# Activations in two tiles, weight copies placed by foresight, and 16-column products alternating with 512-column ones

## The chip, the cores and the metric

One Trainium2 chip, one core. The time is the device time of one execution of the whole kernel in microseconds, the median of several runs.

## The reference

Two transformer-like blocks over 1024 tokens of width 1024, all in float32. The first block puts 16 learned tokens ahead (1040 in all), and computes differential attention beside a state space model, both from one projection:

```python
h = rms_norm(h_res, pre_mix_g)
proj = h @ w_in                       # q1 q2 k1 k2 (partial rope), v, u
o = rms_norm(diff_attention(q1, q2, k1, k2, v, lam), subln_g) * (1 - lam_init)
y = gelu(s5_ssm(u, ...)); y = rms_norm(y * sigmoid(y @ w_glu + b_glu), ssm_out_g)
h_res = h_res + rms_norm(concat(o, y) @ w_out, post_mix_g)
h = rms_norm(h_res, pre_ffn_g)
h_res = h_res + rms_norm((silu(h @ w_gate) * (h @ w_up)) @ w_down, post_ffn_g)
```

The second block works on the 1024 tokens alone: retention beside RWKV-7, an output product, a gated feed-forward of the same kind, and at the end a gated per-layer input. Every dense product is against a weight matrix with 1024 rows (2816 in w_down).

## The kernel before, in words

**Number format.** A float32 operand is held as a high part rounded to the fast format fp32r and a low part (the rest, in the same format). A product is three matmuls by PASSES: high weights by high activations, high weights by low activations, low weights by high activations (L144). The activations of all 1040 tokens are in act_hi and act_lo, each [128, 8, 1040], placed at byte 16512 of a partition one behind the other (L93, L94): row stride 4160 bytes, the first half of the tokens 64 bytes into a row, the second 2048 bytes further.

**Weights.** All weights come as 408 units of 512 KB, [128, 1024], in an order fixed in advance (ORDER), through six slots. SyncE starts the transfer of unit pos into w_raw as soon as TensorE has finished unit pos − 6 (L565 to L570). From unit 30 on (W_START) ScalarE rounds it into w_hi (round_to, L1467; its copy is recorded at the helper's line L697), and GpSimd makes w_lo = w_raw − w_hi (split_to, L577; recorded at L586). TensorE waits for w_lo (w_ready) before the unit's first product. Before unit 30 GpSimd makes both.

**Order of the work.** The text of each engine is written out in one fixed order. Tokens are treated in two halves of 512. Stage 0 (until 560 us) has the first block's norm, projection (project, L1545, then project_far, L1561, whose pieces are mixed with attention), the state space model and attention of half 0. Then come four phases, in each of which a mixing part of one half (attention, or retention and RWKV) is interleaved with a dense part of the other: phase 1 from 561 us, phase 2 from 1196, phase 3 from 2005, and phase 4 (the last dense part alone) from 2900 us. A list of events, EVENTS[1] to EVENTS[4] (L535 to L556), says whether the next step is mixing or dense. Each engine walks the same list: it does its own part of the event and, on ScalarE and GpSimd, then prepares weight units up to a number that the list gives for this event (L1508 to L1517 and L671 to L675). That number is the smaller of "units begun with this event, plus 3" (W_AHEAD) and "units ended three events earlier, plus 6". So a unit is prepared as soon as its slot can have been filled. A list event of a dense product is one quarter of a unit, six matmuls of 512 columns.

**Lines of products.** feature_product (L1610; matmuls at L1617) makes the q and k features of the first projection: per tile m of 128 features eight k steps times three passes, for 512 tokens (s=0) and, for m = 4 to 7, also for the 16 learned tokens (s=2). far_inputs (L1581, L1587) makes the four tiles of u in the same way. rotate (L1635, matmul L1640) makes rope's rotated half from ScalarE's copy qk_raw, which VectorE then combines. dense_products (L1848, matmuls L1855) has weights as stationary operand and activations as moving one; down (matmuls L1884) has the feed-forward's inner values ffh as stationary and weights as moving; token_product (L1891, L1896) has activations stationary and weights moving. Each product's result is copied out of PSUM by ScalarE or VectorE; before a PSUM bank is written again, TensorE waits for the copy (proj_kept in the projection).

**GpSimd's other work.** Besides splitting weights it makes tables at the start, and, in phases 2 and 3, helps RWKV: rw_keys (L600) waits for a transfer of aa and does seven multiplications, all recorded at L598, at 16 places of the list. It stands in GpSimd's order like any event.

Of the kernel before, what the change touches and what calls it, by code (L numbers as in the profile page):

```python
# [14 lines left out]
P = 128  # L15
# [70 lines left out]
def build(nc, t):  # L86
# [6 lines left out]
    act_hi = place("act_hi", [P, KT, L], F32R, AT_ACT)  # L93
    act_lo = place("act_lo", [P, KT, L], F32R, AT_ACT + KT * L * 4)  # L94
# [15 lines left out]
    def tok_cols(i):  # L110
        return slice(META + P * i, META + P * i + P)

# [6 lines left out]
    NEAR = META + BANK  # L119

# [24 lines left out]
    acts, ws = (act_hi, act_lo), (w_hi, w_lo)  # L145
# [411 lines left out]
    assert ended[-1] == len(ORDER)  # L557
    AT = {key: pos for pos, key in enumerate(ORDER)}
# [121 lines left out]
    def _(act):  # L680
# [42 lines left out]
        def first_norm():  # L723

            tiles = tiles_of(0)
            for step in range(len(tiles) + 2):
# [8 lines left out]
                if step >= 2:  # L735
                    g, rows, _, c0 = tiles[step - 2]
                    act.wait_ge(turned, g + 1)
                    if rows == META:
                        give(fn(act_hi[:, :, 0:META], ps[:, 0, 0:KT * META].rearrange("p (k n) -> p k n", k=KT), ACT.Copy), hi_done)
                    else:  # L740
                        for b in range(2):
                            bank = 2 * (g % 2) + b
                            fin = fn(act_hi[:, 4 * b:4 * b + 4, c0:c0 + P], ps[:, bank, :].rearrange("p (k n) -> p k n", k=4), ACT.Copy)
# [187 lines left out]
        def attention(h):  # L931

            def output_high(u):
                pair, qi, hh = unit_of(h, u)
                act.wait_ge(o_turned, HEAD_UNITS * h + u + 1)
                give(fn(act_hi[:, 2 * pair + hh, tok_cols(qi)], ps[:, 7, VD:2 * VD], ACT.Copy), o_hi)
# [43 lines left out]
        def glu(h):  # L980
# [36 lines left out]
            cols = slice(META + BANK * h, META + BANK * h + BANK)  # L1017
            for m in range(4):
                act.wait_ge(glu_prod, 4 * (2 * h + 1) + m + 1)
                give(fn(act_hi[:, 4 + m, cols].rearrange("p (c t) -> p t c", t=OCT), y_raw[:, m], ACT.Copy), glu_hi)  # L1020
# [24 lines left out]
        def mix_norm(h):  # L1045
# [3 lines left out]
            for step in range(NORM_STEPS):  # L1049
# [18 lines left out]
                if step >= 2:  # L1068
                    k = step - 2
                    act.wait_ge(dense_turned, gt_ + k + 1)  # L1070
                    for b in range(2):
                        out = act_hi[:, 4 * b:4 * b + 4, tok_cols(HALF * h + k)]
# [13 lines left out]
        def residual_half(h):  # L1086
# [12 lines left out]
            for step in range(NORM_STEPS):  # L1099
# [17 lines left out]
                if step >= 2:  # L1117
                    g, _, _, c0 = tiles[step - 2]
                    act.wait_ge(turned, g + 1)
                    for b in range(2):  # L1120
                        fin = fn(act_hi[:, 4 * b:4 * b + 4, c0:c0 + P], ps[:, 4 + 2 * (g % 2) + b, :].rearrange("p (k n) -> p k n", k=4), ACT.Copy)
# [101 lines left out]
        def ret_high(i):  # L1223
            act.wait_ge(ret_turned, i + 1)
            give(fn(act_hi[:, 0:4, tok_cols(i)], ps[:, 6, :].rearrange("p (k n) -> p k n", k=4), ACT.Copy), ret_hi)
# [2000 lines left out]
```

## Time and profile before

| what | value |
|---|---|
| median of 3 runs | 3389.66 us (3388.5 to 3397.58) |
| the profiled execution | 3409.39 us, span 3407.6 us |
| mean granted clock of TensorE | 0.943 |
| instructions | 48139, of them 19536 matmuls |
| bytes read from and written to HBM | 281.89 and 44.97 MB, 96 GB/s over the span |

PE is TensorE's matmuls, PEld its weight loads, DVE VectorE, ACT ScalarE, POOL GpSimd, SP SyncE. A profile row of a group gives line, engine, operation, destination and sources by the program's names, count, busy time and mean duration, and after the bar the time that the engine stood idle just before such instructions with what ended most of it. The duration of a matmul is modelled and overlaps with the next; the distance from start to start is its price. The granted clock is 1 at full speed (2.4 GHz) and 0.5 at the lower level (1.2 GHz).

### The profile page before, as it was taken

To read this page: it belongs to the slowest core of one execution; us is meant where nothing else is said; L and a number is where in the kernel's file an instruction comes from. 1 tells how busy PE (TensorE), PEld (TensorE's weight loads), DVE (VectorE), ACT (ScalarE), POOL (GpSimd) and SP (SyncE) were. 2 spreads that over 40 slices of the span, in tenths; PEclk is the share of its full clock that TensorE was granted. 3 is DMA by queue.
4 is the path that set the end of the run, shared out by engine and by line. 5 is a ranking of instruction groups with operands and counts; after the bars stand their busy time and mean duration, and the time that the engine had idled before them with its cause. 6 is when DMAs were issued, how large, how long until landed. Compare 5 with 4: busy or idle time off the path is not lost.

```text
span 3407.6 us, 48139 instructions
## 1 busy us (share of the span) xinstructions
PE 3105.6 (91%) x19536; PEld 2396.3 (70%) x19536; DVE 1506.9 (44%) x2264; ACT 1225.1 (36%) x1969; POOL 1232.6 (36%) x698
## 2 busy tenths in 40 slices
PE   6997877898998889989999989998999989899997
PEld 4775655676766666877777767777777767788875
DVE  5844542443443461355555553435455554222233
ACT  3111214533432463243444344343434443322232
POOL 5811302132322323434444332434444432344432
PEclk9887888899999889999999999999999989999998
DMA  4343323222212254332222243332222222322231
GB/s 152 118 119 94 104 78 106 87 74 87 69 62 71 77 187 152 103 99 86 75 76 84 72 155 133 129 103 81 84 74 86 78 72 82 123 93 96 90 105 56
DMA packets 158030, 330.02 MB, mean 97 GB/s; under 512 B 34960, under 2 KB 74064, under 8 KB 157808
## 3 DMA queue, kind: packets, MB, share of 16 engines
q1 hardware_dynamic: 58752, 213.94, 18.8%
q10 hardware_dynamic: 99056, 112.99, 10.2%
q8 instruction: 155, 2.54, 0.3%
q14 instruction: 67, 0.55, 0.0%
HBM read 281.89 MB, written 44.97 MB: 96 GB/s over the span
## 4 chain that ended last, share of the span: by engine, by line
PE 79%; DVE 12%; ACT 3%; ACTq 2%; issue 2%; DMA 1%; POOL 0%; DVEq 0%; POOLq 0%
PE ps L1855 34%; PE ps L1896 13%; PE ps L1884 12%; PE ps L1706 2%; PE ps L1617 2%; DVE acc_dense L2291 2%; PE ps L1587 1%; DVE ffh_lo L2971 1%; PE ps L2090 1%; ACTq L988 1%; PE ps L1627 1%; DVE act_lo L2291 1%; PE ps L1734 1%; PE ps L1794 1%; PE ps L1982 1%
## 5 line engine op out<-in xcount | busy, mean ns | idle before, releaser
L586 POOL TENSOR_TENSOR w_lo<-w_raw,w_hi 128x1024 fp32r<-128x1024 f32 x408 | 999.5, 2460 | 1735.1 <-ACT w_hi L697 1731.4
L1855 PE MATMUL ps<-act_hi,w_hi 128*128 128x512 f32 x1696 | 701.5, 414 | 13.6 <-ACT qk_raw L697 8.1
L1855 PE MATMUL ps<-act_lo,w_hi 128*128 128x512 f32 x1696 | 677.2, 399 | 0.0
L1855 PE MATMUL ps<-act_hi,w_lo 128*128 128x512 f32 x1696 | 673.6, 397 | 0.0
L697 ACT ACTIVATE w_hi<-w_raw 128x1024 fp32r<-128x1024 f32 x378 | 390.2, 1052 | 152.8 <-DMA w_raw<-weights 75.2
L1855 PEld LDWEIGHTS ps<-act_hi,w_hi 128*128 128x128 f32 x1696 | 322.5, 190 | 108.4 <-issue 16.6
L1855 PEld LDWEIGHTS ps<-act_hi,w_lo 128*128 128x128 f32 x1696 | 323.0, 190 | 74.6
L1855 PEld LDWEIGHTS ps<-act_lo,w_hi 128*128 128x128 f32 x1696 | 322.5, 190 | 66.7 <-issue 1.7
L1884 PE MATMUL ps<-w_hi,ffh_hi 128*128 128x512 f32 x704 | 297.2, 422 | 60.8 <-DVE acc_dense L2291 57.4
L2291 DVE TENSOR_TENSOR acc_dense<-acc_dense,ps 128x512 f32<-128x512 f32 x352 | 242.1, 688 | 228.5 <-PE ps L1884 182.3
L1896 PE MATMUL ps<-w_hi,act_hi 128*128 128x512 f32 x640 | 261.5, 409 | 26.7 <-POOL w_lo L586 11.9
L1884 PE MATMUL ps<-w_hi,ffh_lo 128*128 128x512 f32 x704 | 284.0, 403 | 0.0
L1884 PE MATMUL ps<-w_lo,ffh_hi 128*128 128x512 f32 x704 | 283.0, 402 | 0.0
L1896 PE MATMUL ps<-w_hi,act_lo 128*128 128x512 f32 x640 | 258.0, 403 | 0.0
L1896 PE MATMUL ps<-w_lo,act_hi 128*128 128x512 f32 x640 | 255.3, 399 | 0.0
L2967 DVE TENSOR_TENSOR ff_f<-ff_f,ps 128x512 f32<-128x512 f32 x88 | 60.5, 688 | 392.0 <-PE ps L1855 391.4
L1884 PEld LDWEIGHTS ps<-w_hi,ffh_hi 128*128 128x128 f32 x704 | 137.6, 195 | 103.1 <-DVE acc_dense L2291 65.8
L692 ACT ACT_TABLE_LOAD x141 | 180.9, 1283 | 32.8 <-issue 24.5
L1896 PEld LDWEIGHTS ps<-w_hi,act_hi 128*128 128x128 f32 x640 | 123.7, 193 | 61.1 <-issue 21.9
L1884 PEld LDWEIGHTS ps<-w_lo,ffh_hi 128*128 128x128 f32 x704 | 137.5, 195 | 31.2
L697 ACT ACTIVATE ff_f<-ps 128x512 f32<-128x512 f32 x88 | 52.7, 598 | 291.0 <-PE ps L1855 289.8
L1884 PEld LDWEIGHTS ps<-w_hi,ffh_lo 128*128 128x128 f32 x704 | 137.7, 196 | 25.9
(372 smaller groups left out, 4284.7 us busy)
## 6 DMA issues: line engine op xcount, KB each, us to landing
w_raw<-weights SPq DMA_DIRECT2D x408, 512.0 KB, 3.5
rw<-rw_t ACTq DMA_DIRECT2D x24, 256.0 KB, 2.3
rw<-lora_t ACTq DMA_DIRECT2D x24, 256.0 KB, 2.0
row<-x ACTq DMA_DIRECT2D x8, 512.0 KB, 3.7
row_dense<-x ACTq DMA_DIRECT2D x8, 512.0 KB, 6.1
row_mix<-res ACTq DMA_DIRECT2D x8, 512.0 KB, 8.0
res<-row_mix ACTq DMA_DIRECT2D x8, 512.0 KB, 4.2
acc_dense<-res ACTq DMA_DIRECT2D x8, 512.0 KB, 5.2
```

What stands on the lines that cost most here:

```text
L586: pool.tensor_tensor(w_lo[:, s], raw, w_hi[:, s].bitcast(F32), SUB).then_inc(w_ready, 1)
L692: act.preload_act_table_set(SETS[func])
L697: return act.activation(out, in_, func, **kw)
L988: act.dma_start(y_raw[SG * j:SG * j + SG, m], y_view[:, :, 8 * m + j, c0:c0 + BANK // OCT]).then_inc(y_landed, 16)
L1587: mm = pe.matmul(ps[:, n % 2, 0:c1 - c0], ws[w][:, pos % SLOTS, P * k:P * k + P], acts[a][:, k, c0:c1], start=(k, w, a) == (0, 0, 0), stop ...
L1617: mm = pe.matmul(ps[:, n % 3, 0:c1 - c0], ws[w][:, u % SLOTS, P * k:P * k + P], acts[a][:, k, c0:c1], start=(k, w, a) == (0, 0, 0), stop=( ...
L1706: mm = pe.matmul(out[:, c:c + w], q, k[:, META + c:META + c + w], start=True, stop=True)
L1855: mm = pe.matmul(out, ws[w][:, s, P * k:P * k + P], acts[a][:, k, x], start=(k, w, a) == (0, 0, 0), stop=(k, w, a) == (KT - 1, 1, 0))
L1884: mm = pe.matmul(ps[:, 2 + n % 2, :], ffh[a][:, m % 4, P * k:P * k + P], ws[w][:, s, BANK * j:BANK * j + BANK], start=(m % 2, w, a) == (0, ...
L1896: mm = pe.matmul(ps[:, kinds[2] + k, :], source[a][:, 2 * uu + kk, x], ws[w][:, pos % SLOTS, BANK * kk:BANK * kk + BANK], start=(uu, kk, w ...
L2291: give(dve.tensor_tensor(out, a, b, op), signal)
L2967: give(dve.tensor_tensor(ff_f[:, m % 2], ff_f[:, m % 2], ps[:, 1, :], MUL), ff_prod)
```

## The change

1. **Layout.** act_hi and act_lo are replaced by tiles in the same bytes: for the first block's projection near_hi and near_lo, [128, 8, 528], hold the 16 learned and the first 512 tokens, and half_acts[h], [128, 8, 512], hold a half each. half_acts[0] overlays the near tiles (it is written when they are done with). All reads and writes of activations go through these.
2. **Copies with foresight.** The number of units that ScalarE and GpSimd prepare after an event is worked out with a look at the units that begin up to six events later.
3. **Alternation.** feature_products and far_inputs make the 512-column and the 16-column product of a tile together, changing from one to the other at each weight tile; PE's waits for a free bank move accordingly.

The core of the diff:

```diff
-    act_hi = place("act_hi", [P, KT, L], F32R, AT_ACT)
-    act_lo = place("act_lo", [P, KT, L], F32R, AT_ACT + KT * L * 4)
+    near_acts, half_acts = [], ([], [])
+    for n, name in enumerate(("hi", "lo")):
+        at = AT_ACT + n * KT * L * 4
+        near_acts.append(place(f"near_{name}", [P, KT, NEAR], F32R, at))
+        for h in range(2):
+            half_acts[h].append(place(f"act_{name}_{h}", [P, KT, BANK], F32R, at + h * KT * NEAR * 4))
...
-    W_START, W_AHEAD, W_BEHIND = len(ORDER), 3, 4
-    EVENTS, ended, made_ready = {}, [W_START] * W_BEHIND, [W_START + W_AHEAD]
+    W_START, W_AHEAD, W_BEHIND, W_LOOK = len(ORDER), 3, 3, 6
+    EVENTS, begun, ended = {}, [], [W_START] * W_BEHIND
     def event(side, h, starts, ends):
         ORDER.extend((h, u) for u in starts)
-        assert len(ORDER) <= made_ready[-1]
+        begun.append(len(ORDER))
         ended.append(ended[-1] + len(ends))
-        made_ready.append(min(len(ORDER) + W_AHEAD, ended[-W_BEHIND] + SLOTS))
-        return side, made_ready[-1]
+        return side, len(begun) - 1
+
+    def weights_by(e):
+        soon = begun[min(e + W_LOOK, len(begun) - 1)]
+        return max(begun[min(e + 1, len(begun) - 1)], min(soon, begun[e] + W_AHEAD, ended[e + 1] + SLOTS))
...
             for n, (kind, m, s) in enumerate(PROJ):
-                if n >= 3:
-                    pe.wait_ge(proj_kept, n - 2)
+                ahead = len(spans_of(m)) - 1 if kind == "qk" else 0
+                if n + ahead >= 3 and s != 2:
+                    pe.wait_ge(proj_kept, n + ahead - 2)
                 if kind == "v":
                     value_product(n, m)
-                else:
-                    feature_product(n, m, s)
+                elif s != 2:
+                    feature_products(n, m)
...
-                free = len(PROJ) + n - (kind != "qk")
-                if n:
+                free = len(PROJ) + n - (kind != "qk" and s != 0)
+                if n and s != 2:
                     pe.wait_ge(proj_kept, free)
...
-            for k in range(KT) if s == 2 else range(2 * part, 2 * part + 2):
+            for k in range(2 * part, 2 * part + 2):
                 for w, a in PASSES:
-                    mm = pe.matmul(ps[:, n % 2, 0:c1 - c0], ws[w][:, pos % SLOTS, P * k:P * k + P], acts[a][:, k, c0:c1],
-                                   start=(k, w, a) == (0, 0, 0), stop=(k, w, a) == (KT - 1, 1, 0))
-            if s == 2 or part == 3:
-                post(mm, unit_done if s == 1 else proj_psum)
+                    for of, (c0, c1) in enumerate((SPANS[0], SPANS[2]) if s == 0 else (SPANS[1],)):
+                        mm = pe.matmul(ps[:, (n + of) % 2, 0:c1 - c0], ws[w][:, pos % SLOTS, P * k:P * k + P], first_cols(a, k, c0, c1 - c0),
+                                       start=(k, w, a) == (0, 0, 0), stop=(k, w, a) == (KT - 1, 1, 0))
+                        if (k, w, a) == (KT - 1, 1, 0):
+                            post(mm, unit_done if s == 1 else proj_psum)
...
-        def feature_product(n, m, s):
-
-            u, (c0, c1) = AT[0, U_QK + m], SPANS[s]
-            if s == 0:
-                pe.wait_ge(w_ready, u + 1)
+        def feature_products(n, m):
+
+            u = AT[0, U_QK + m]
+            pe.wait_ge(w_ready, u + 1)
             for k in range(KT):
                 for w, a in PASSES:
-                    mm = pe.matmul(ps[:, n % 3, 0:c1 - c0], ws[w][:, u % SLOTS, P * k:P * k + P], acts[a][:, k, c0:c1],
-                                   start=(k, w, a) == (0, 0, 0), stop=(k, w, a) == (KT - 1, 1, 0))
-            post(mm, unit_done if ends_unit("qk", m, s) else proj_psum)
+                    for of, s in enumerate(spans_of(m)):
+                        c0, c1 = SPANS[s]
+                        mm = pe.matmul(ps[:, (n + of) % 3, 0:c1 - c0], ws[w][:, u % SLOTS, P * k:P * k + P], first_cols(a, k, c0, c1 - c0),
+                                       start=(k, w, a) == (0, 0, 0), stop=(k, w, a) == (KT - 1, 1, 0))
+                        if (k, w, a) == (KT - 1, 1, 0):
+                            post(mm, unit_done if ends_unit("qk", m, s) else proj_psum)
```

## Rows read from the trace of the kernel before

**Rows 1.** The page, busy time of each engine: us, share of the span, instructions.

```profile
PE 3105.6 (91%) x19536; PEld 2396.3 (70%) x19536; DVE 1506.9 (44%) x2264; ACT 1225.1 (36%) x1969; POOL 1232.6 (36%) x698
```

**Rows 2.** Windows of two stages; columns: us, engines' busy us (count), PEclk, DMA share, GB/s.

```profile
1196.00:2005.00 809.00, 766.62 (x6347) 594.15 (x6348) 396.20 (x586) 334.35 (x518) 324.95 (x208) 0.98 0.30 101
2005.00:2900.00 895.00, 839.63 (x6654) 655.26 (x6653) 421.14 (x612) 364.82 (x559) 346.72 (x218) 0.97 0.30 100
```

**Rows 3.** Windows of four stretches at a low granted clock, columns as before.

```profile
127.00:137.00 10.00, 10.00 (x45) 7.01 (x45) 9.69 (x10) 1.53 (x4) 9.45 (x9) 0.51 0.50 157
...
164.00:172.00 8.00, 8.00 (x28) 6.58 (x28) 1.19 (x4) 0.18 (x1) 3.26 (x2) 0.57 0.27 99
178.00:192.00 14.00, 8.38 (x18) 5.54 (x19) 4.83 (x8) 0.00 (x0) 4.57 (x2) 0.51 0.43 131
216.00:226.00 10.00, 10.00 (x29) 7.28 (x28) 2.97 (x6) 0.94 (x4) 0.00 (x0) 0.50 0.11 27
```

**Rows 4.** Timeline of PE, 3019 to 3035 us: start, us, engine, line, operation.

```profile
3019.79 0.39 PE L1855 MATMUL ps<-act_hi,w_lo 128*128 128x512 f32 x1
...
3028.36 0.40 PE L1884 MATMUL ps<-w_hi,ffh_hi 128*128 128x512 f32 x1
...
3034.49 0.39 PE L1884 MATMUL ps<-w_hi,ffh_hi 128*128 128x512 f32 x1
```

**Rows 5.** The page, groups of section 5.

```profile
L1855 PE MATMUL ps<-act_hi,w_hi 128*128 128x512 f32 x1696 | 701.5, 414 | 13.6 <-ACT qk_raw L697 8.1
...
L1855 PEld LDWEIGHTS ps<-act_lo,w_hi 128*128 128x128 f32 x1696 | 322.5, 190 | 66.7 <-issue 1.7
...
L1896 PE MATMUL ps<-w_hi,act_hi 128*128 128x512 f32 x640 | 261.5, 409 | 26.7 <-POOL w_lo L586 11.9
```

**Rows 6.** Timeline of PE, a run of 24 products of 16 columns.

```profile
147.46 0.26 PE L1617 MATMUL ps<-act_hi,w_lo 128*128 128x16 f32 x1
147.57 0.35 PE L1617 MATMUL ps<-act_hi,w_hi 128*128 128x16 f32 x1
147.77 0.36 PE L1617 MATMUL ps<-act_lo,w_hi 128*128 128x16 f32 x1
```

**Rows 7.** Timeline of PE, the end of the projection's rotations.

```profile
184.57 0.58 PE L1640 MATMUL ps<-qk_raw,rot 128*128 128x16 f32 x2 [3.99 <-DVE qk_raw L2291]
```

**Rows 8.** Tile w_hi on ACT: its instructions, what they waited for (us, times).

```profile
L697 ACT ACTIVATE w_hi<-w_raw x378: 1037/1050/1066, 553.9 to 3358.9; 128x1024 fp32r<-128x1024 f32 x189
...
  DMA w_raw<-weights: 75.2, 16
```

**Rows 9.** The chain in order of time: start us, us, what; and ACT's timeline, 617 us.

```profile
2013.88 1.06 ACT w_hi L697
...
617.60 1.06 ACT L697 ACTIVATE w_hi<-w_raw 128x1024 fp32r<-128x1024 f32 x1 [3.03 <-DMA w_raw<-weights]
```

**Rows 10.** Timeline of POOL and PE around two late units; the group of POOL's first key product.

```profile
1848.75 2.38 POOL L586 TENSOR_TENSOR w_lo<-w_raw,w_hi 128x1024 fp32r<-128x1024 f32 x1
...
1844.39 0.40 PE L1855 MATMUL ps<-act_hi,w_hi 128*128 128x512 f32 x1
...
2702.65 2.39 POOL L586 TENSOR_TENSOR w_lo<-w_raw,w_hi 128x1024 fp32r<-128x1024 f32 x1
...
2699.01 0.40 PE L1855 MATMUL ps<-act_hi,w_hi 128*128 128x512 f32 x1
...
L598 POOL TENSOR_TENSOR kk<-kraw,rw_vec_s 128x256 f32<-128x256 f32 x16 | 10.8, 678 | 41.7 <-DMA aa<-rw 41.7
```

**Rows 11.** Timeline of ACT and PE, the unit of 1152.5 us.

```profile
1151.34 1.06 ACT L697 ACTIVATE w_hi<-w_raw 128x1024 fp32r<-128x1024 f32 x1
...
1152.51 0.80 PE L1855 MATMUL ps<-act_hi,w_hi 128*128 128x512 f32 x1
```

**Rows 12.** Waits of PE: for whom, us in total, times, longest.

```profile
PE ps L1884 <- DVE acc_dense L2291: 57.4, 25, 12.1
...
PE ps L1896 <- POOL w_lo L586: 11.9, 2, 11.7
```

More of the change, by code:

```diff
@@ L119, in build, with of_tile, first_cols @@
     NEAR = META + BANK
+    near_acts, half_acts = [], ([], [])
[4 more added lines that the diff above has]
+            half_acts[h].append(place(f"act_{name}_{h}", [P, KT, BANK], F32R, at + h * KT * NEAR * 4))
+    def of_tile(part, ks, i):
+        return half_acts[i // HALF][part][:, ks, P * (i % HALF):P * (i % HALF) + P]
+    def first_cols(part, ks, c0, rows):
+        if c0 < NEAR:
+            return near_acts[part][:, ks, c0:c0 + rows]
+        return half_acts[1][part][:, ks, c0 - NEAR:c0 - NEAR + rows]
     row = place("row", [P, 3, D], F32, ARENA)
@@ L144, in build @@
     PASSES = ((0, 0), (0, 1), (1, 0))
-    acts, ws = (act_hi, act_lo), (w_hi, w_lo)
+    ws = (w_hi, w_lo)
     def tiles_of(c):
@@ L557, in build @@
     assert ended[-1] == len(ORDER)
+    assert all(weights_by(e) <= ended[e + W_BEHIND] + SLOTS for e in range(len(begun)))
+    EVENTS = {phase: [(side, weights_by(e)) for side, e in events] for phase, events in EVENTS.items()}
     AT = {key: pos for pos, key in enumerate(ORDER)}
@@ L738, in first_norm @@
                     if rows == META:
-                        give(fn(act_hi[:, :, 0:META], ps[:, 0, 0:KT * META].rearrange("p (k n) -> p k n", k=KT), ACT.Copy), hi_done)
+                        give(fn(near_acts[0][:, :, 0:META], ps[:, 0, 0:KT * META].rearrange("p (k n) -> p k n", k=KT), ACT.Copy), hi_done)
                     else:
@@ L935, in output_high @@
                 act.wait_ge(o_turned, HEAD_UNITS * h + u + 1)
-                give(fn(act_hi[:, 2 * pair + hh, tok_cols(qi)], ps[:, 7, VD:2 * VD], ACT.Copy), o_hi)
+                give(fn(of_tile(0, 2 * pair + hh, qi), ps[:, 7, VD:2 * VD], ACT.Copy), o_hi)
             if h == 0:
@@ L1224, in ret_high @@
             act.wait_ge(ret_turned, i + 1)
-            give(fn(act_hi[:, 0:4, tok_cols(i)], ps[:, 6, :].rearrange("p (k n) -> p k n", k=4), ACT.Copy), ret_hi)
+            give(fn(of_tile(0, slice(0, 4), i), ps[:, 6, :].rearrange("p (k n) -> p k n", k=4), ACT.Copy), ret_hi)
         def mark(ins, sem, value):
@@ L1291, in rw_high @@
             act.wait_ge(rw_norm, nth("norm", "out", v))
-            give(fn(act_hi[:, 4 + 2 * s:6 + 2 * s, tok_cols(i)], yo[:, :, :], ACT.Copy), mix_hi)
+            give(fn(of_tile(0, slice(4 + 2 * s, 6 + 2 * s), i), yo[:, :, :], ACT.Copy), mix_hi)
         def rwkv(h):
@@ L1626, in value_product @@
                 for w, a in PASSES:
-                    mm = pe.matmul(ps[0:rows, n % 3, :], acts[a][:, k, c0:c0 + rows],
+                    mm = pe.matmul(ps[0:rows, n % 3, :], first_cols(a, k, c0, rows),
                                    ws[w][:, AT[0, U_V + k // 2] % SLOTS, BANK * (k % 2):BANK * (k % 2) + BANK],
@@ L1846, in first_dense, with dense_products @@
             yield from feed_forward(0, h)
-        def dense_products(pos, out, part, x, last):
+        def dense_products(pos, out, part, h, last):
             s = pos % SLOTS
@@ L2406, in output_low @@
             dve.wait_ge(o_hi, HEAD_UNITS * h + u + 1)
-            out = (slice(None), 2 * pair + hh, tok_cols(qi))
-            tt(act_lo[out], ps[:, 7, VD:2 * VD], act_hi[out].bitcast(F32), SUB, o_lo)
+            tt(of_tile(1, 2 * pair + hh, qi), ps[:, 7, VD:2 * VD], of_tile(0, 2 * pair + hh, qi).bitcast(F32), SUB, o_lo)
         def attention(h):
@@ L2879, in rw_low @@
             take(mix_hi)
-            where = (slice(None), slice(4 + 2 * s, 6 + 2 * s), tok_cols(i))
-            tt(act_lo[where], yo[:, :, :], act_hi[where].bitcast(F32), SUB, mix_lo)
+            where = (slice(4 + 2 * s, 6 + 2 * s), i)
+            tt(of_tile(1, *where), yo[:, :, :], of_tile(0, *where).bitcast(F32), SUB, mix_lo)
         def rwkv(h):
```

67 lines of the change are left out of this document (32 added, 35 removed).

## The prediction

> **What bounds the kernel now.** I read the page first, then stages, then the engines that feed TensorE (PE). PE is busy 91% of the span, ScalarE (ACT) and GpSimd (POOL) 36% each [rows 1], and the chain of waits that ended last is mostly PE's own work. From 1196 to 2900 us the windows show PE busy in 766.62 of 809 and 839.63 of 895 us at granted clocks of 0.98 and 0.97, so 98 us are idle there [rows 2]. So whatever shortens a matmul is gained, and whatever makes PE wait is lost unless it falls into those idle times. The start is different: between 127 and 226 us the clock stands five times near 0.5, its lower level of 1.2 GHz, for 8 to 14 us each. VectorE (DVE) is busy in 9.69 of 10 us in the first of these stretches, as in the second (147 to 158 us, which has no row of its own), and in 1.19 of 8 in the third [rows 3]. All sums are made against the profiled execution, 3409.4 us (span 3407.6), 19.7 us above the median of the runs, 3389.7; I move the median by the same difference. About 0.3% (10.2 us) is what a measurement of this kernel tells from no change.
>
> **Layout.** It adds and removes no instruction: every read of an activation has a new address, all half tiles start at the same offset in 512 bytes, rows are 2048 bytes instead of 4160. The products by activations and the down products do the same work, yet not at one pace. From 3019.79 to 3028.36 us 37 starts of L1855 take 8.57 us, 231.6 ns each; from 3028.36 to 3034.49 us 27 starts of L1884, whose stationary operand lies above 155 KB, take 6.13 us, 227.0 ns [rows 4]. So operand addresses have a price of up to 5 ns. There are 3 x 1696 products at L1855 and 3 x 640 at L1896 [rows 5]. In L1855 the starts sorted by their place in 256 bytes already show what the new place does: a triple of passes takes 690.9 ns where the tile starts as all will after the change, against 696.2 ns on average (worked out from the starts of that line, of which [rows 4] holds a stretch); in L1896 the same sorting gives no difference. So 1696 x 5.3 ns = 9 us, less the tenth of them at the lower clock, where the sorting shows nothing: **−8 us**. Ends: all 7008 products go to 227 ns, 7008 x 5 ns = −35 us; and +5 us, because half the range of offsets is new together with a new row stride. I take the value of the sorted rows, since they are the same line with the same weights.
>
> The Trainium skill, page SBUF — State Buffer, section Who interferes with whom, gives PE two independent read ports, one for the moving operand and one for the weights, and sees no contention there. By that rule this term would be 0 and the whole sum 8 us higher; the 4.6 ns between the two lines above speak against it.
>
> **Alternation.** 192 products of 16 columns in eight runs of 24 are put between products of 512 columns. None is removed, and each keeps its own weight load: the two passes by w_hi stand side by side today, and both loads are in the trace, 1696 for each of the three products of L1855 [rows 5]. A product of 16 columns starts 0.11 us after the last [rows 6], so by itself the alternation costs 227 + 112 ns a pair, as now. If the second load of a pair were hidden, 192 x 0.112 = 21.5 us would go. What does change is the clock. It falls during the 16-column run that began at 145.23: up to 147.57 the starts are 0.11 us apart, then 0.20 [rows 6]. Five of the eight runs are followed by such a fall, and in the windows each lasts 8 to 14 us [rows 3]. At full clock 10 us of PE's work take 5. The first two are covered by DVE, the fourth has PE busy only 8.38 of 14 us [rows 3]; the third and the fifth (8 and 10 us, PE busy throughout) could give 4 and 5. Against it: the rotations of an m whose 16-column product was their cover have nothing before them; one that has nothing before it today stands 3.99 us for DVE [rows 7], and I count 2 us for two of them, since part of DVE's work is done by then. The first far u product of a tile waits for one copy more (of 16 columns), which is within the same 4 us. Two steps of the ssm stand next to each other on PE now and carry nothing that waits. I take 9 + 3 (a part of the fourth) − 4: **−8 us**. Ends: −25 us (all five stretches shortened) and +8 us (clock as before, each uncovered rotation and copy paid twice).
>
> **Copies with foresight, the gain.** A weight unit's rounding (ACT, L697, 1050 ns, 378 times [rows 8]) is now put at the event six before its first use, where before it went as soon as three earlier events had ended. Walking the two plans over the kernel's event list, 312 of 378 copies come later, 1 earlier, 65 at the same place; their lead in events falls from mostly 12 to 18 to 6 (318 of them). ACT stood 75.2 us before 16 copies until their transfer had landed [rows 8], with everything behind them in ACT's order standing too. Nearly all is hidden. On the chain of waits it shows once fully: the transfer of its unit, then the copy, 1.06 us, ahead of the norm's squares that PE's next product needs [rows 9]; with the copy later, ACT's 3.03 us of idle time [rows 9] and the 1.06 us go. A second copy on the chain stands at 2013.88 us [rows 9]. Two or three more copies stand in front of norm steps whose chain runs through DVE, so they give less than their length. 4 + 1 + 3: **−8 us**, ends −2 and −15.
>
> **Copies with foresight, the cost.** The chain of a unit is copy 1.05, low part on POOL (L586) 2.4 us [rows 10], with the hops 3.7 us. Today it ends a median of 15.9 us before PE needs the unit. With a lead of six events I took, for each unit, the time at which ACT and POOL passed the event that now releases it, added 3.7 us (or POOL's part), and compared with PE's first use. 49 of 378 come too late, from unit 36 at 589.8 to unit 325 at 2896.2 us. Two patterns:
> - POOL does the keys of RWKV (seven multiplications, 5.6 us with their gaps) after waiting for a transfer, 41.7 us in 16 such places. At one it has come to the split only at 1848.75; PE starts on that unit at 1844.39, so 1848.75 + 2.38 is 6.7 us late. The same at 2702.65 + 2.39, with PE at the unit at 2699.01, gives 6.0 us [rows 10]. Ten such places sum to 29 us.
> - ACT passes the event just before PE needs the unit: copy at 1151.34, PE's use at 1152.51; 1151.3 + 3.7 is 2.5 us late [rows 11]. Such places sum to 23 us.
>
> Counting each place once that is 52 us (81 if every unit were paid singly). SP's queue of transfers isn't touched: it waits for PE's uses alone. Nobody else waits for w_lo. How much of the 52 us ends in the time is the open question. PE waits for others in the same stretches, for DVE's acc_dense 57.4 us in 25 places [rows 12], and a PE that comes late to such a wait loses nothing twice. ACT also sheds the copies that stood ahead of its mixing work, so it passes an event up to 1 us sooner for each. And places that follow closely (four from 1460 to 1511 us) are paid once. I take a quarter: **+12 us**. Ends 0 and +52.
>
> **Sum.** −8 −8 −8 +12 = −12: profiled 3397, median **3377.7 us**.
>
> **Rivals.**
> 1. *The new waits are paid* (slower, 0.36). POOL's keys and ACT's lag hold the units; PE meets them as waits on w_lo at L1855, L1884 and L1896, mostly 1500 to 2900 us. All of it: −24 + 52 = +28, 3418 us. It decides from 34 us of new waits on (34 − 24 = 10). For it: the 6.7 and 6.0 us above are bare differences of two rows, and PE is 94% busy there. Against it: the idle times that stand behind.
> 2. *The parts cancel* (0.20): 24 us of new waits, or neither layout nor clock gives anything and few waits are paid; 3390 us.
> 3. *The layout does more* (0.08, within faster): all products reach 227 ns, −35 −8 −8 +12 = −39, 3351 us. For it: the pace of L1884. Against it: only one of three transitions reached 227 in the sorted rows.
> 4. *The alternation doesn't keep the clock*: it does not do what it says, its term is 0 to +8, and the other terms give −4 to +4, that is 3386 to 3394. This holds half of the chance of rival 2; where more of the waits are absorbed too, it stays in the likeliest case.
>
> **How the numbers follow.** The likeliest case, the gains with a quarter of the waits, gets 0.36, its own range 3362 to 3379; with rival 3 faster is 0.44. Within 0.3% 0.20, slower 0.36. The range: below, rival 3 at 3351; above, rival 1 in full at 3418; beyond lie some 0.1 each.
>
> **What would show it.** Layout right: starts of L1855 230 ns apart or less, wrong if 232. Alternation right: no window at 0.5 between 127 and 226 us, and DVE's wait before the last rotation no longer than 3.99 us. Foresight right: the copy near 617 us behind the squares, ACT's wait for transfers before copies far under 75 us. Its cost: PE's waits on POOL w_lo, now 11.9 us in 2 places [rows 12], stay under 30 in my case and exceed 45 in rival 1, the longest near the units at 1844 and 2699 us. I would be wrong if these waits exceed the other gains, or if the products of L1855 slow down.

## The result, and the profile after

| | median us | ratio to before |
|---|---|---|
| before | 3391.56 | 1 |
| after | 3473.41 | 1.0235 (95% interval 1.0214 to 1.0256) |

The change costs 82 us, 2.4%. I had forecast 3377.7 with a range up to 3418. (The first profiled execution of the changed kernel was a disturbed one of 7428 us; everything below of "after" is read from a second one, of 3466.8 us span, from a series of runs that gave a ratio of 1.0246, 1.0220 to 1.0272.)

The page of after, busy times and one group; the lines are those of the changed kernel, where dense_products is L1877 (L1855 before), down L1903 (L1884) and token_product L1915 (L1896):

```profile
PE 3108.5 (90%) x19536; PEld 2416.9 (70%) x19536; DVE 1487.7 (43%) x2264; ACT 1224.2 (35%) x1969; POOL 1222.8 (35%) x698
...
L1877 PE MATMUL ps<-act_hi,w_hi 128*128 128x512 f32 x1696 | 702.0, 414 | 56.8 <-POOL w_lo L604 42.4
```

The work is the same: 19536 products, PE busy 3108.5 us against 3105.6 [rows 1]. Span less busy time is 358 us against 302, so 56 of the 59 us between the two profiled spans are idle time of PE, and no new work. The busy sum hides two changes that cancel, as experiment 1 shows: faster products and a lower clock. The mean granted clock is 0.934, in the profile of before 0.943; the other runs of before have 0.945 to 0.955, so that profile, which took 3409.4 us against a median of 3391.6, makes the difference look smaller than it is. In L1877 the idle time before the first product of a unit is 56.8 us, against 13.6 [rows 5], now by POOL's w_lo.

Who PE waited for, after (us in total, times, longest):

```profile
PE ps L1877 <- POOL w_lo L604: 42.4, 14, 7.3
...
PE ps L1903 <- DVE acc_dense L2310: 24.2, 9, 7.9
PE ps L1903 <- POOL w_lo L604: 21.7, 13, 4.0
PE ps L1915 <- POOL w_lo L604: 20.2, 8, 11.7
```

Waits on w_lo are 84 us, against 11.9 [rows 12]; those on acc_dense went from 57.4 to 24.2. Some of the new waits stand where PE would have waited for DVE.

Windows of after, columns as in [rows 2]:

```profile
127.00:137.00 10.00, 9.63 (x61) 7.32 (x60) 8.54 (x9) 2.87 (x7) 9.37 (x10) 0.83 0.49 170
164.00:172.00 8.00, 8.00 (x24) 5.88 (x22) 0.00 (x0) 0.78 (x2) 0.00 (x0) 0.50 0.07 9
...
200.00:270.00 70.00, 64.81 (x205) 53.71 (x205) 15.14 (x48) 7.03 (x15) 0.00 (x0) 0.50 0.22 69
...
1196.00:2005.00 809.00, 744.12 (x6036) 582.05 (x6035) 383.61 (x574) 329.76 (x507) 315.02 (x205) 0.97 0.31 101
2005.00:2900.00 895.00, 826.57 (x6597) 647.90 (x6598) 410.27 (x611) 356.31 (x540) 343.41 (x218) 0.96 0.30 97
```

The first two are stretches of [rows 3]: 0.83 and 0.50 against 0.51 and 0.57. The third is the finding: from 200 to 270 us the clock is at 0.50 throughout, with PE busy 64.81 of 70 us. The same window of the kernel before, at 0.83 and with 287 products in place of 205:

```profile
200.00:270.00 70.00, 61.70 (x287) 48.24 (x287) 30.44 (x77) 13.76 (x35) 12.78 (x6) 0.83 0.43 105
```

In the two long stages PE is busy in 744.12 of 809 and 826.57 of 895 us, 36 us less than in [rows 2] for the same length (the work has moved to later times, so the windows don't hold quite the same products): most of the waits on w_lo are there.

The pace of dense products, timeline of PE, after, the first and last of 178 products of which no record is missing:

```profile
3019.42 0.40 PE L1877 MATMUL ps<-act_hi,w_lo 128*128 128x512 f32 x1
...
3059.60 0.39 PE L1877 MATMUL ps<-act_hi,w_lo 128*128 128x512 f32 x1
```

(3059.60 − 3019.42) / 177 = 227.0 ns a product against 231.6 [rows 4]. So the layout gave more than forecast, and the other two parts cost.

The late unit of [rows 10] in after, first POOL, then PE, then ACT's waits before its copies (us, times):

```profile
1884.47 0.61 POOL L616 TENSOR_TENSOR kk<-kraw,rw_vec_s 128x256 f32<-128x256 f32 x1 [8.16 <-DMA aa<-rw]
...
1889.91 4.65 POOL L604 TENSOR_TENSOR w_lo<-w_raw,w_hi 128x1024 fp32r<-128x1024 f32 x2
```

```profile
1884.70 0.40 PE L1877 MATMUL ps<-act_hi,w_lo 128*128 128x512 f32 x1
1892.40 0.77 PE L1877 MATMUL ps<-act_hi,w_hi 128*128 128x512 f32 x1 [7.30 <-POOL w_lo L604]
```

```profile
  DMA w_raw<-weights: 10.2, 2
```

POOL waits 8.16 us for its transfer, makes its keys until 1889.8, and then splits; PE stands 7.30 us. ACT's waits for transfers fell from 75.2 to 10.2 us, as the plan should do.

### The profile page after: what moved, and what is told of

Read it like the earlier page. It is cut to its first block, busy times and chain, and to the rows that moved or that the text cites. A ratio compares the mean times of both kernels' runs of the same rounds, so it can differ in the third digit from the quotient of the medians.

```text
span 7426.1 us, 48155 instructions
## 1 busy us (share of the span) xinstructions
PE 7266.5 (98%) x19536; PEld 4345.1 (59%) x19536; DVE 1375.6 (19%) x2264; ACT 1228.0 (17%) x1969; POOL 1196.1 (16%) x698
## 4 chain that ended last, share of the span: by engine, by line
PE 97%; DVE 1%; ACT 1%; ACTq 0%; issue 0%; DMA 0%; POOL 0%; DVEq 0%; POOLq 0%
PE ps L1877 41%; PE ps L1903 17%; PE ps L1915 16%; PE ps L1728 2%; PE ps L1607 2%; PE ps L1638 2%; PE ps L1756 1%; PE ps L2109 1%; PE ps L1649 1%; PE ps L2001 1%; PE ps L1816 1%; PE ps L1618 1%; PE ps L1713 1%; PE ps L2172 1%; PE ps L2209 1%; PE ps L2094 1%
## 5 line engine op out<-in xcount | busy, mean ns | idle before, releaser
L1877 PE MATMUL ps<-act_hi,w_hi 128*128 128x512 f32 x1696 | 1435.6, 846 | 9.3 <-DVE act_lo L2310 5.5
L1877 PE MATMUL ps<-act_hi,w_lo 128*128 128x512 f32 x1696 | 1398.6, 825 | 0.0
L1877 PE MATMUL ps<-act_lo,w_hi 128*128 128x512 f32 x1696 | 1398.5, 825 | 0.0
L1877 PEld LDWEIGHTS ps<-act_hi,w_hi 128*128 128x128 f32 x1696 | 578.9, 341 | 443.4 <-issue 393.4
L1877 PEld LDWEIGHTS ps<-act_hi,w_lo 128*128 128x128 f32 x1696 | 597.5, 352 | 391.5 <-issue 376.7
L1877 PEld LDWEIGHTS ps<-act_lo,w_hi 128*128 128x128 f32 x1696 | 607.6, 358 | 347.3 <-issue 347.3
L1903 PE MATMUL ps<-w_hi,ffh_hi 128*128 128x512 f32 x704 | 590.3, 838 | 2.2 <-DVE acc_dense L2310 2.2
L1903 PE MATMUL ps<-w_hi,ffh_lo 128*128 128x512 f32 x704 | 580.8, 825 | 0.0
L1903 PE MATMUL ps<-w_lo,ffh_hi 128*128 128x512 f32 x704 | 580.1, 824 | 0.0
L1915 PE MATMUL ps<-w_hi,act_hi 128*128 128x512 f32 x640 | 533.1, 833 | 25.1 <-POOL w_lo L604 16.1
L1915 PE MATMUL ps<-w_lo,act_hi 128*128 128x512 f32 x640 | 529.6, 828 | 0.0
L1915 PE MATMUL ps<-w_hi,act_lo 128*128 128x512 f32 x640 | 529.1, 827 | 0.0
L1903 PEld LDWEIGHTS ps<-w_lo,ffh_hi 128*128 128x128 f32 x704 | 249.3, 354 | 161.0 <-issue 154.5
L1903 PEld LDWEIGHTS ps<-w_hi,ffh_hi 128*128 128x128 f32 x704 | 238.8, 339 | 169.0 <-issue 162.6
L1903 PEld LDWEIGHTS ps<-w_hi,ffh_lo 128*128 128x128 f32 x704 | 251.9, 358 | 144.5 <-issue 144.5
L1915 PEld LDWEIGHTS ps<-w_hi,act_hi 128*128 128x128 f32 x640 | 222.2, 347 | 186.4 <-issue 178.2
L1915 PEld LDWEIGHTS ps<-w_lo,act_hi 128*128 128x128 f32 x640 | 225.6, 353 | 154.0 <-issue 151.8
L1915 PEld LDWEIGHTS ps<-w_hi,act_lo 128*128 128x128 f32 x640 | 226.2, 353 | 146.3 <-issue 146.3
```

Source lines behind the costliest of these rows:

```text
L1877: mm = pe.matmul(out, ws[w][:, s, P * k:P * k + P], half_acts[h][a][:, k, :], start=(k, w, a) == (0, 0, 0), stop=(k, w, a) == (KT - 1, 1, 0))
L1903: mm = pe.matmul(ps[:, 2 + n % 2, :], ffh[a][:, m % 4, P * k:P * k + P], ws[w][:, s, BANK * j:BANK * j + BANK], start=(m % 2, w, a) == (0, ...
L1915: mm = pe.matmul(ps[:, kinds[2] + k, :], source[a][:, 2 * uu + kk, x], ws[w][:, pos % SLOTS, BANK * kk:BANK * kk + BANK], start=(uu, kk, w ...
```

## The experiments

**1. The three parts alone.** One kernel of each, and after once more.

Layout alone is the diff's first part; foresight alone is this on the kernel before:

```diff
-        made_ready.append(min(len(ORDER) + W_AHEAD, ended[-W_BEHIND] + SLOTS))
...
+        soon = begun[min(e + W_LOOK, len(begun) - 1)]
+        return max(begun[min(e + 1, len(begun) - 1)], min(soon, begun[e] + W_AHEAD, ended[e + 1] + SLOTS))
```

and alternation alone is feature_products, far_inputs and the waits of project and project_far.

> The changed kernel once more, since the only profile of it shows every matmul of 512 columns at about 0.82 us and can't be laid beside the kernel before. About 3473 us, 2.4% above the kernel before. Theory W (the foresight's new waits are paid): PE's waits on w_lo sum to some 80 us, the starts of L1877 stay at 231 ns. Theory L (the layout slows the products): waits on w_lo stay near 12 us and the starts of L1877 and L1915 come some 11 ns later each, 7008 x 11 ns = 77 us. Theory C (more of the span at the lower clock): the mean granted clock falls by 1% from 0.943 and neither waits nor the pace at full clock change.

> The kernel before with the new activation tiles alone. Theory W: 3382 us (-8, as predicted) and in any case within 10 us of the kernel before. Theory L: 3460 us or more, starts of L1855's products at 240 ns or more. Theory C: between, with more of the span at half clock.

> The kernel before with the new plan of weight copies alone. Theory W: 3440 to 3470 us, PE's waits on w_lo 50 to 80 us, longest near the units first used at 1844 and 2699 us. Theory L: 3385 to 3400 us, waits on w_lo under 25 us.

> The kernel before with 16-column and 512-column products alternating, nothing else. Theories W and L: 3380 to 3400 us, all the difference before 310 us of the span. Theory C: slower, with PE at 0.5 for more than the five stretches of before between 127 and 226 us.

| kernel | median us | ratio (95%) |
|---|---|---|
| after again | 3473.47 | 1.0246 (1.0220 to 1.0272) |
| layout alone | 3369.97 | 0.9937 (0.9916 to 0.9959) |
| foresight alone | 3438.51 | 1.0139 (1.0117 to 1.0161) |
| alternation alone | 3443.13 | 1.0154 (1.0124 to 1.0185) |

Their product is 0.9937 x 1.0139 x 1.0154 = 1.0230, the whole 1.0246: the parts add. In microseconds of 3392: −21, +47, +52. Theory L is out, the layout is a gain. W is right with its part: waits on w_lo of 79.8 us were in its window of 50 to 80, the time 1.5 us below its 3440. Where it put the other two kernels (3382 us, and 3380 to 3400 for the alternation) it was wrong. C (clock) is right with the alternation, and neither explains all. The pages show the split: span less PE's busy time is 303 us with the layout, 307 with the alternation and 341 with the foresight, against 302 before, and PE is busy 3061.8, 3145.2 and 3094.6 us, against 3105.6. The foresight costs idle time, the alternation busy time.

Foresight alone, who PE waited for:

```profile
PE ps L1861 <- POOL w_lo L592: 39.0, 14, 6.7
...
PE ps L1890 <- DVE acc_dense L2297: 25.1, 9, 8.2
PE ps L1902 <- POOL w_lo L592: 20.7, 7, 11.7
PE ps L1890 <- POOL w_lo L592: 20.1, 13, 3.9
```

39.0 + 20.7 + 20.1 = 79.8 us on w_lo, 68 more than before, in 34 places where before had 2; acc_dense gives 32 back. One of the places, PE's timeline:

```profile
1849.98 0.76 PE L1861 MATMUL ps<-act_hi,w_hi 128*128 128x512 f32 x1 [6.74 <-POOL w_lo L592]
1850.54 0.63 PE L1861 MATMUL ps<-act_lo,w_hi 128*128 128x512 f32 x1
1850.97 0.63 PE L1861 MATMUL ps<-act_hi,w_lo 128*128 128x512 f32 x1
...
1854.84 0.39 PE L1861 MATMUL ps<-act_hi,w_hi 128*128 128x512 f32 x1
1855.07 0.40 PE L1861 MATMUL ps<-act_lo,w_hi 128*128 128x512 f32 x1
```

It stood 6.74 us, and the walk over the old rows had said 6.7 for this unit. The duration and distance of the next products show something I had left out: starts 0.43 us apart at first (1850.54, 1850.97), 0.23 only from 1854.84. PE comes back from this wait at the lower clock, runs some 4.9 us at half pace and so loses 2.4 us more. The timeline shows such slow products behind nine of the 34 waits, the longer ones, some 28 us of them in all against 5.5 us before; at half pace that is about 11 us of loss beside the waits (my estimate). Behind the short waits there are none.

Alternation alone, windows:

```profile
120.00:130.00 10.00, 9.63 (x66) 6.56 (x64) 9.65 (x11) 1.94 (x4) 9.45 (x9) 1.00 0.40 117
130.00:140.00 10.00, 10.00 (x43) 8.10 (x42) 8.47 (x9) 1.52 (x4) 9.45 (x9) 0.55 0.32 115
...
220.00:230.00 10.00, 8.55 (x29) 7.08 (x28) 0.00 (x0) 1.28 (x2) 0.00 (x0) 0.50 0.32 106
290.00:300.00 10.00, 10.00 (x47) 7.30 (x46) 5.05 (x8) 2.52 (x6) 3.46 (x2) 1.00 0.78 210
```

and PE's timeline, each row a pair of a 512- and a 16-column product:

```profile
219.23 0.79 PE L1590 MATMUL ps<-act_hi,w_lo 128*128 128x512 f32 x2
219.87 0.79 PE L1590 MATMUL ps<-act_hi,w_hi 128*128 128x512 f32 x2
```

0.64 us a pair: at the lower clock 427 + 213. From 130 to 288 us the clock never comes back. Before, it came back after each of its five falls. Nor is PE held by others: it is busy 8.55 of the 10 us from 220 on, the other 1.45 us are one wait for ACT's copy u_t, and it is just slow. (This profile took 3454.3 us, against a median of 3443.1.)

**2. Which pairs, and where the fall begins.** q and k alone, far u alone, and the whole alternation with the projection's events rearranged:

```diff
-    PROJ_EVENTS = ["proj", "ssm"] + ["proj"] * 5 + ["ssm", "proj"] * TB + ["proj"] * 5
+    PROJ_EVENTS = ["proj", "ssm"] + ["proj"] * 4 + ["ssm", "proj"] * 5 + ["proj", "ssm", "proj"] * 3 + ["proj"] * 3
```

> Alternation in the q and k products alone, the far u products as before. With the whole alternation TensorE stands at 0.50 from 130 to 288 us without coming back, and the kernel before comes back after each of its five falls. Theory P (a fall is ended only by plain 512-column products in a row, and 512 and 16 in turn don't count as such): 3402 to 3412 us, clock 0.50 from 130 to some 190 us, back to full in the far products that come in a row of their own. Theory Q (the far part alone costs): within 5 us of the kernel before.

> Alternation in the far u products alone. Theory P: 3415 to 3430 us, 0.50 from about 186 to 288 us. If the alternation in q and k is what holds the clock down for both, 3385 to 3395 us.

> The whole alternation, and the list of events of the projection changed so that every step of the state space model (64x16 and 16x16 products) again has a projection product on either side; in the alternation as made, two pairs of these steps follow each other, and the clock falls at the end of the first pair, at 130.8 us. Theory R (the small steps side by side cause the fall, and pairs of 512 and 16 columns keep a full clock if they start with it): the clock stays at 1.00 through 130 to 190 us, 3395 to 3415 us in all. Theory P: the clock falls in the first pairs anyway and stays down to 288 us, 3435 to 3450 us.

| kernel | median us | ratio (95%) |
|---|---|---|
| q and k alone | 3414.47 | 1.0057 (1.0038 to 1.0075) |
| far u alone | 3417.14 | 1.0072 (1.0048 to 1.0095) |
| whole, events rearranged | 3436.98 | 1.0150 (1.0113 to 1.0187) |

Both places cost about the same. For the far part P has it (3415 to 3430 us; the clock is at 0.50 from 180 to 250 us, though not to the 288 it had said). For q and k it hasn't: the time is 2.5 us above its 3402 to 3412, and the clock doesn't stay at 0.50 from 130 to 190 us. A window of q and k alone, and PE's timeline just before it, each row a pair:

```profile
160.00:170.00 10.00, 7.59 (x43) 5.98 (x41) 3.13 (x10) 0.78 (x2) 0.00 (x0) 1.00 0.31 107
```

```profile
158.84 0.79 PE L1619 MATMUL ps<-act_hi,w_hi 128*128 128x512 f32 x2
159.48 0.62 PE L1619 MATMUL ps<-act_lo,w_hi 128*128 128x512 f32 x2
159.96 0.49 PE L1619 MATMUL ps<-act_hi,w_lo 128*128 128x512 f32 x2
```

The clock rises in the fifth pair after a row of state space steps, and the pairs then run 0.34 us apart to the end of their tile. So P is too strong: pairs can see the clock rise. But where they began at the lower clock, at 132.1 and at 170.3 us, all 24 pairs of a tile stayed there, 15 us each. (This profile took 3401.0 us at a mean granted clock of 0.951, the other five runs 3411 to 3419 at 0.942 to 0.946, so they may have had less of the full clock.) The rearranged kernel, windows:

```profile
120.00:140.00 20.00, 20.00 (x131) 15.81 (x129) 19.42 (x17) 3.47 (x8) 18.90 (x17) 1.00 0.38 129
...
170.00:280.00 110.00, 99.03 (x306) 78.88 (x306) 29.54 (x74) 11.15 (x26) 6.22 (x3) 0.50 0.20 62
```

The clock is 1.00 through the first pairs, up to 140 us, where alternation alone stood at 0.55 from 130 on: the fall went with the small steps side by side, and the pairs kept the full clock that they began with, so R is right about the place. But its 3395 to 3415 us are missed, the time is the same. A fall comes some 18 us later, behind a wait of 4.97 us for DVE's qk_raw, it ends once more at 157 us, again within a few pairs after state space steps, a wait of 2.41 us and the next fall follow, and from 170 to 280 us the clock is at 0.50. What costs is less how a fall begins than that it doesn't end.

**3. The same far products, grouped.** Within each quarter first six products of 512 columns, then six of 16, laid here against the far part as made:

```diff
-            for k in range(2 * part, 2 * part + 2):
-                for w, a in PASSES:
-                    for of, (c0, c1) in enumerate(...):
+            for of, (c0, c1) in enumerate(...):
+                for k in range(2 * part, 2 * part + 2):
+                    for w, a in PASSES:
```

> Alternation in the far u products alone, but within each quarter first six products of 512 columns, then six of 16, instead of one by one; the same products, the same waits. Theory P1 (the clock doesn't come back because every second product is short): it comes back within the first tile, 0.5 for less than 20 us after 185, 3390 to 3402 us. Theory P2 (what counts is how much of a quarter is short products, whatever their order): 0.50 from about 180 to 255 us again, 3412 to 3420 us.

Measured: 3396.09 us, ratio 1.0025 (1.0007 to 1.0043), 21 us under the far part as made and inside P1's window. Windows of the far part, one by one (the stretches between are alike), then grouped:

```profile
190.00:200.00 10.00, 8.55 (x29) 7.08 (x27) 0.00 (x0) 2.56 (x3) 0.00 (x0) 0.50 0.64 236
...
220.00:230.00 10.00, 10.00 (x31) 8.46 (x32) 8.06 (x18) 0.00 (x0) 0.00 (x0) 0.50 0.11 27
```

```profile
190.00:200.00 10.00, 9.10 (x36) 7.73 (x35) 0.00 (x0) 2.57 (x3) 0.00 (x0) 0.68 0.92 322
200.00:210.00 10.00, 9.90 (x58) 8.34 (x56) 2.15 (x11) 1.49 (x5) 0.00 (x0) 1.00 0.11 29
...
220.00:230.00 10.00, 9.84 (x58) 8.35 (x58) 4.74 (x10) 1.05 (x5) 0.00 (x0) 1.00 0.12 27
```

0.50 from the first 10 us of the u products to the last against 0.68 and then 1.00; in the grouped kernel the clock rises at 196.3 us, 11 us after the first of them. The products, weights, the waits that are written and the share of short products in a quarter are the same; only the order is different. P1 holds here: in the far products the clock stays down because every second product is a short one.

**4. The foresight: lead, or something else.** New layout and plan, W_LOOK 12 instead of 6:

> New layout and new plan of copies, but with a look of 12 events instead of 6; no alternation. If the cost of the foresight is the lead alone (replayed: the latest of the late units was 6.7 us late, twelve events of a dense stretch take some 17 us against 8): waits on w_lo back near 12 us, and 3360 to 3372 us, that is the layout's 3370 less what copying later spares ACT. If the plan costs in another way: 3390 us or more.

Measured: 3374.97 us, ratio 0.9939 (0.9914 to 0.9965). Who PE waited for, and ACT's wait for transfers before its copies:

```profile
PE ps L1852 <- DVE xn_dense L2312: 43.3, 15, 8.6
PE ps L1898 <- DVE acc_dense L2305: 38.4, 18, 11.9
...
PE ps L1910 <- POOL w_lo L604: 13.5, 3, 11.7
```

```profile
  DMA w_raw<-weights: 28.0, 6
```

w_lo is back at 13.5 + 1.1 us. So the lead of six events is the whole cost, as far as the intervals tell. The time is 3 us above the 3360 to 3372 that I expected, and that of the layout alone (0.9937): ACT's waits for transfers went from 75 to 28 us, and nothing came of it. acc_dense fell from 57.4 to 38.4 us, xn_dense rose from 39.3 to 43.3. The gain I had put at 8 us can't be seen; the intervals allow some 10 us either way.

**5. Whose fault the late units are.** The keys of RWKV two mixing events later in POOL's order, on the old plan and on the new:

```diff
-                if v + 1 in vs:
-                    rw_keys(v + 1)
-                for _ in range(8):
-                    yield
+                for _ in range(2):
+                    yield
+                if v + 1 in vs:
+                    rw_keys(v + 1)
+                for _ in range(6):
+                    yield
```

> The kernel before, with GpSimd's RWKV keys from the second unit on two mixing events later in its order (14 of the 16 places), so that their transfer has landed when it comes to them. Both theories: what the displacement costs or gives by itself, 3385 to 3405 us; no wait on w_lo in phases 2 and 3.

> The new plan of copies alone, with the same displacement. Against foresight alone at 3438.5 us. Theory K: the six waits of 3 to 7 us on w_lo in phases 2 and 3 fall to 3 us or less, the sum from 80 to 45 us or less, and the time comes to 3405 to 3420 us if the displacement alone is neutral. Theory A: the waits stay within 10 us of 80 in sum, the time at 3435 to 3445 us.

| kernel | median us | ratio (95%) |
|---|---|---|
| keys later, old plan | 3397.51 | 1.0017 (1.0000 to 1.0035) |
| keys later, new plan | 3403.16 | 1.0032 (1.0018 to 1.0046) |
| new plan, keys in place | 3438.51 | 1.0139 (1.0117 to 1.0161) |

Who PE waited for with the new plan and the keys later:

```profile
PE ps L1904 <- POOL w_lo L592: 20.9, 7, 11.7
PE ps L1863 <- POOL w_lo L592: 19.9, 8, 6.1
...
PE ps L1892 <- POOL w_lo L592: 14.4, 12, 3.9
```

79.8 us on w_lo became 55.2, and 35 us of the 47 went. By time K is right, its window of 3405 to 3420 even too high. By waits it is only half right: I expected 45 or less and no long one, and waits of 6.1 and 5.6 us are left (the first unit of each half has its keys unmoved; POOL stands 16.9 us before them there). Between the two profiles 26 us of PE's idle time went and 12.5 us of its busy time (3094.6 to 3082.1 us, at a granted clock of 0.949 and 0.954). Slow products behind waits on w_lo fell from some 28 to 18 us, which explains about 5 us of that; the rest isn't settled.

**6. What in an address sets the pace.** The tiles of half 0 moved by 64 or by 256 bytes, half 1 in place, on the layout alone:

```diff
-            half_acts[h].append(place(f"act_{name}_{h}", [P, KT, BANK], F32R, at + h * KT * NEAR * 4))
+            half_acts[h].append(place(f"act_{name}_{h}", [P, KT, BANK], F32R, at + h * KT * NEAR * 4 + 64 * (1 - h)))
```

> The new layout alone, with the tiles of half 0 moved by 64 bytes; those of half 1 stay where they are and serve as the comparison inside one run. Theory S (the start address of an operand sets the pace, 228.2 ns a product at 128 in 512 bytes against 232 mixed): half 0's products of L1866's line go to 231 to 234 ns, half 1's stay at 228; the time is 8 to 14 us above the new layout's 3370. Theory T (the row stride of 2048 instead of 4160 bytes sets it): both halves stay at 228, 3370 us.

> As before it, but half 0 moved by 256 bytes, to 384 in 512. The kernel before has this place at k=3 and k=7, where the three transitions took 226.7, 234.8 and 229.5 ns, 230.3 on average. If the place in 512 bytes counts: those three numbers in half 0, 4 to 7 us above the new layout. If only the place in 256 bytes counts: 228 in both halves, 3370 us, and the sorted rows of before were something else.

Measured: 3374.26 us, 0.9949 (0.9932 to 0.9967) with 64 bytes; 3364.31 us, 0.9932 (0.9907 to 0.9957) with 256. With intervals that overlap the times alone decide nothing (S had asked for 3378 us or more with 64 bytes), the timelines do. PE in the kernel moved by 64 bytes, ends of a stretch of retention products of half 0, then of half 1:

```profile
1349.31 0.39 PE L1904 MATMUL ps<-w_hi,act_lo 128*128 128x512 f32 x1
...
1436.34 0.40 PE L1904 MATMUL ps<-w_lo,act_hi 128*128 128x512 f32 x1
...
2139.26 0.40 PE L1904 MATMUL ps<-w_hi,act_lo 128*128 128x512 f32 x1
...
2225.89 0.39 PE L1904 MATMUL ps<-w_lo,act_hi 128*128 128x512 f32 x1
```

87.03 us over 373 starts is 233.3 ns, 86.63 over 382 is 226.8: same line, same work, same run. Half 0's products are in phase 2 and half 1's in phase 3, but that isn't it: in the layout alone those of phase 2 take 226.8. With 256 bytes the stretch of half 0 takes 226.8 too (starts taken as above). So the start address of the activation operand sets the pace here (theory S), and 256 bytes more leave it as it is; whether 128 would too was not tried. For dense_products the difference in half 0 is smaller, 229.5 against 227.7 ns as a mean of its products in phase 1, not the 231 I expected, and less than the 231.6 before; how much the row stride adds there stays open.

**7. A version that beats both.** The 16 learned tokens in a tile of their own, so that half 0 is aligned in the first projection too; old plan, no alternation:

> The new layout carried on: the 16 learned tokens in a tile of their own, so that half 0 is one tile for the first projection too and its products there start at the same place in 512 bytes. Old plan of copies, no alternation. Theory S: 288 products at L1628's and L1638's lines and 96 at the far u go from 231.7 to 228, 1.5 us less than the new layout alone: 3368 us, 0.7% below the kernel before. Theory T: 3370 us or above.

```diff
-        near_acts.append(place(f"near_{name}", [P, KT, NEAR], F32R, at))
+        near_acts.append(place(f"near_{name}", [P, KT, META], F32R, at))
...
-            half_acts[h].append(place(f"act_{name}_{h}", [P, KT, BANK], F32R, at + h * KT * NEAR * 4))
+            half_acts[h].append(place(f"act_{name}_{h}", [P, KT, BANK], F32R, at + KT * META * 4 + h * KT * BANK * 4))
...
-        if c0 < NEAR:
+        if c0 < META:
             return near_acts[part][:, ks, c0:c0 + rows]
+        if c0 < NEAR:
+            return half_acts[0][part][:, ks, c0 - META:c0 - META + rows]
```

Measured: 3364.26 us, ratio 0.9926 (0.9908 to 0.9943): below the kernel before by 0.7% and below after by 3.1%. Against the layout alone it is inside the intervals, so the time doesn't decide between S and T. The timeline shows the products of the first projection at 228.5 ns (L1630) where the layout alone has 231.6 (L1628); start and row stride of their tile both changed, so either could be the reason.

## Why the prediction was wrong

**Forecast −12 us, measured +82.** Term by term:

- **Layout, −8, ends −35 and +5.** Measured −21 (0.9937). Right in direction, too small. The step that failed is the sorting of the starts of L1855 by their place in 256 bytes: I took 690.9 ns for a triple as what it would be after the change. Each of those aligned products stood between unaligned ones, which is the likely reason, though not shown; with all aligned a product takes 226.7 (phase 4) to 229.2 ns (phase 2), a triple 680 to 688 and not 690.9; and the retention and output products, which the same sorting had shown unchanged, gained as much as the others (231.7 to 226.8 ns in phase 2). The better sign stood in [rows 4]: the dense products came to the pace of the down products, in phase 4 to 226.7 ns both. The Trainium skill, page SBUF — State Buffer, section Who interferes with whom, gives PE two independent read ports and would have let one expect nothing; here 64 bytes of displacement are worth 6.5 ns a product within one run, and the measurement decides. That the two ports disturb each other isn't shown by it, only that an operand's start matters.
- **Alternation, −8, ends −25 and +8.** Measured +52 (1.0154), outside my own ends. The failed step is "what does change is the clock": I counted the five falls and the PE time in them, and took it for granted that the runs of short products cause them and that mixing them in removes the cause. I bounded the other side by "clock as before". The trace of before had what ends a fall. All five of those around [rows 3] end amid plain 512-column products, for instance the third, timeline of PE before:

```profile
171.11 0.58 PE L1617 MATMUL ps<-act_lo,w_hi 128*128 128x512 f32 x1
171.52 0.39 PE L1617 MATMUL ps<-act_hi,w_lo 128*128 128x512 f32 x1
171.75 0.39 PE L1617 MATMUL ps<-act_hi,w_hi 128*128 128x512 f32 x1
```

Setting a short product behind each of those took the recovery from the far part (experiment 3) and mostly from q and k (experiment 2). The prices of the pair (0.64 us at the lower clock, as 427 + 213) were right. The two neighbouring ssm steps, of which I wrote that they carry nothing that waits, do go with the first fall; the rearranged kernel, without that fall but with a wait of 4.97 us, took the same time.
- **Foresight's gain, −8, ends −2 and −15.** Nothing measurable. The step "on the chain it shows once fully" took ACT's idle time ahead of a copy for time of the kernel. ACT's waits did go (75 to 10 or 28 us), and the squares near 617 us no longer stand behind a copy. But PE's waits for the norms, on xn_dense, didn't fall: 39.3 us before, 41.2 with the foresight alone and 43.3 with the look of 12. A gain of the 8 us forecast isn't excluded by the intervals, only not seen.
- **Foresight's cost, +12, ends 0 and +52.** Measured +47 for gain and cost together. The walk over the rows was right, almost unit by unit (6.7 and 6.0 us forecast, 6.74 and 5.93 measured at 1850 and 2715 us); the sum was 52 and became 68. The failed step is "I take a quarter". The argument that existing waits for DVE would swallow them holds for 32 of 68 us at most. I set against it no count of how many late places stand directly before such a wait; and the longer waits add products at the lower clock, an estimated 11 us. Rival 1 had this right but for the 52 us.

The rivals: 1 was the side that came true, with its mechanism, but it holds only half of the loss; 4 had its place (the clock) and not its size. No case had both at once, and none had the clock getting worse than before, so the range stopped at 3418. My signs to look for were useful: that the waits on w_lo "exceed 45 in rival 1" and "no window at 0.5 between 127 and 226 us" point straight to the two causes. The sign for the foresight, ACT's waits far under 75 us, came true and was worth nothing that can be seen.

## What to carry to other kernels

- Where the clock is concerned, ask of each stretch not only what makes it fall but what lets it rise again, and don't take those products away. Here a block of short products cost one fall of 8 to 14 us; one after each long product, they left the clock down for whole tiles once it had fallen.
- A plan that prepares data "just in time" must be laid against every engine's fixed order: one blocking wait on a helper engine ahead of the preparation is a wait of the main engine. When rows give such lateness unit by unit, count it in full and take off only what a named later wait absorbs.
- Give the operands of fast products one good start address (here 128 bytes past a multiple of 256), and compare lines that do the same work at a different pace: the faster line tells what the slower can reach.

## What the runs showed of the hardware that I had not expected

- With 512- and 16-column products in turn the granted clock stayed at 0.50 for over 100 us (170 to 280, PE busy 99.03 of 110 us). In the far part alone, the same products in groups of six saw it rise 11 us after the first. Pairs that began at full clock kept it (134 to 142 us in the rearranged kernel), and in q and k alone it rose once amid pairs, at 159.5 us.
- Moving a moving or stationary fp32r operand by 64 bytes changes 512-column products from 226.8 to 233.3 ns where activations are stationary, and by about 2 ns where they are moving; 256 bytes change neither.
- After a wait of 6.74 us PE's next products start 0.43 us apart for about 5 us, then 0.23 again.
